# A convolved feed-forward network whose up projection is made token-major and turned back by VectorE and a trip through DRAM

## The chip, the cores and the metric

The kernel runs on one core of a Trainium2 chip. The metric is the device time of one execution in microseconds (us). All weights are read from the chip's memory (DRAM) once, in blocks of 1 MB.

## The reference, cut to what matters

Two transformer blocks act on 256 tokens of width 1024. The part that changes is the convolved feed-forward network at the end of the first block:

```python
def conv_ffn(h, w_up, conv_w, conv_b, w_down):       # h: 256 x 1024, w_up: 1024 x 5632
    u = causal_dwconv(h @ w_up, conv_w) + conv_b     # 3 taps along the tokens, per feature
    a, b = jnp.split(u, 2, axis=-1)                  # 2816 features each
    return (jax.nn.silu(a) * b) @ w_down             # w_down: 2816 x 1024
```

It comes behind memory attention (`mem_o`) and a norm (`norm_ffn`). Behind it come the second block's first gated network (`ffn1`, `down1`), whose up and gate projections have the same sizes but no convolution, a token mixer, a second gated network (`ffn2`, `down2`) and a last projection.

## The kernel before

**Blocks and splits.** Every matrix product is made of three products of two-part numbers: high by high, low by high, high by low. SyncE (the queue SP) loads a weight block of 1 MB in two halves of 512 KB into RAW (two slots). ScalarE copies each half to HI (L1656), VectorE subtracts it to LO (L2238), and TensorE uses HI and LO (rings of four blocks). `PHASES` gives the order of the blocks: `up` has 22, `down` 11. `split_ahead(phase, Turn(j))` on ScalarE and on VectorE makes HI and LO of the block four further on: ScalarE waits until block j has been used (`block_done`) and until the raw half has landed. The load of block n waits until LO of block n-2 exists (`lo_is_ready(sp, phase, t, -RAWS, half)`), and each engine and each queue runs strictly in the order in which its program is written.

**Two ways to multiply.** `f_gemm` is feature-major: the weights are the stationary operand and 256 tokens are moved, so that the result has features on partitions and tokens along the free axis, 48 matmuls of 256 columns for a block. `t_half` and `t_open` are token-major: the tokens are stationary (two tiles of 128) and 512 weight columns are moved, 24 matmuls of 512 columns for a block; two blocks (the halves of the contraction) make a chunk of 512 features, for two banks of PSUM. The convolution runs along the tokens, so it wants the feature-major form.

**up before.** Its first three blocks are computed token-major by `f_open` in a second set of PSUM banks (the first tile of tokens needs no second half of the norm), copied to OPENED and turned by TensorE. The other 19 are feature-major. For each block pair (256 features of a, the same of b), `up_step` does on ScalarE two base activations per block (`L2036`, middle tap and bias), a Silu, and the copy to HH; on VectorE four taps per block (`L2726`, straight from PSUM), a gate product (`L2735`) and the low half HL (`L2712`). Steps from the third on are a hardware loop (`repeat`).

**ffn1, for comparison.** It is token-major (`glu`, `glu_steps`): five chunk pairs of gate and up (20 blocks), then two feature-major blocks. VectorE turns the gated product in blocks of 32x32 into TURNED (L2761), SP sends that to DRAM (`hidden_out`, L620) and brings it back into BLOCKS as four transfers (`hidden_in`, L628), ScalarE copies it to HH and VectorE makes HL (L2768). One such round trip belongs to four weight blocks.

**PSUM.** There are four accumulator banks, ACCP 0 to 3. A chunk takes a pair of them, by turns 0 and 1, or 2 and 3; of the two feature-major blocks at the end of ffn1, the first takes bank 0 and the second bank 3. `down` takes all four, 0 and 1 for the first tile of tokens and 2 and 3 for the second; for its first two blocks PE does both blocks of the first tile before the second tile. `acc_banks_free` on PE waits for whoever reads a bank to say that it is taken.

Of the kernel before, what the change touches and what calls it, by code (L numbers as in the profile page):

```python
# [22 lines left out]
P = 128  # L23
# [51 lines left out]
T_OPEN = {"mix_v": 4, "ple_g": 4, "ffn1": 4, "ffn2": 4}  # L75
F_OPEN = {"up": 3}
# [12 lines left out]
GLUS = ("ffn1", "ffn2")  # L89


def _accumulations():
# [9 lines left out]
    for phase, count in PHASES:  # L102
# [8 lines left out]
        elif phase == "w_out":  # L111
            acc(phase, 0, count - 1, 2, 3, 0, 1)
        elif phase in ("mem_o", "down", "down1", "mix_o", "down2"):
            acc(phase, 0, count - 1, 0, 1, 2, 3)
        elif phase in GLUS:
            for q in range(2 * GLU_CHUNKS):
                acc(phase, q, 2 * q + 1, 2 * (q % 2), 2 * (q % 2) + 1)
            for j in range(GLU_T, count):
                acc(phase, j, j, 3 * (j - GLU_T))
        elif phase == "ple_e":  # L120
            pass
        elif phase == "pool":
            for j in range(4):
                acc(phase, j, 0, j)
        else:
            for j in range(count):
                acc(phase, j, j, (j + (phase == "up") * 2) % 4)
# [13 lines left out]
def open_turns(r, phase):  # L141

    norms = norm_turns(r)
    blocks = [f"{phase}.{t}{b}" for t in range(NT) for b in range((F_OPEN[phase] + 1) // 2)]
    return norms[:2] + blocks[:1] + norms[2:] + blocks[1:]

# [11 lines left out]
SMALL += open_turns("norm_ffn", "up") + norm_turns("norm_f1")  # L160
# [3 lines left out]

BY_BLOCK = {f"{phase}.1{b}": FIRST[phase] + min(2 * b + 2, n) for phase, n in F_OPEN.items() for b in range((n + 1) // 2)}
BY_BLOCK["ple.1b"] = FIRST["ple_e"] + 1
# [35 lines left out]
def build(nc, A, out):  # L202
# [24 lines left out]
    with ctx:  # L227
# [94 lines left out]
        UA = at("UA", 44, [P, 2, 2, SEQ])  # L322
        UB = at("UB", 48, [P, 2, 2, SEQ])
# [4 lines left out]
        OPENED = at("OPENED", 56, [P, NT, 4 * 256])  # L328
# [51 lines left out]
        opened = sem("opened")  # L380
# [26 lines left out]
        a_base, a_act, b_base, h_ready, h_hi, h_lo = sems("a_base a_act b_base h_ready h_hi h_lo")  # L407
        turned, turned_out, blocks_in, blocks_split = sems("turned turned_out blocks_in blocks_split")
        post_sq, tap_done, dve_mix = sems("post_sq tap_done dve_mix")
# [25 lines left out]

        def repeat(eng, first, last, stride, step):


            groups, over = divmod(last - first, stride)
            for j in range(first, first + over):  # L440
                step(Turn(j))
            with eng.Fori(0, groups) as i:
                for j in range(first + over, first + over + stride):
                    step(Turn(j, i, stride))
# [34 lines left out]
        def acc_is_done(eng, phase, t):  # L479

            if t.j < F_OPEN.get(phase, 0):
                before = list(F_OPEN.values())[:list(F_OPEN).index(phase)]
                eng.wait_ge(opened, sum(before) + t.j + 1)
                return
# [24 lines left out]
        def conv_tap(tap, tile, t):  # L509

            return FCONV[:, moved(tap * 2 * FT + tile, t, 2)]

        def conv_bias(tile, t):
            tile_, row = COL_AT["ffn_conv_b"]
            return COL[tile_][:, moved(row + tile, t, 2)]

        def moved(c, t, per_turn):

            return slice(c, c + 1) if t.i is None else bass.ds(c + t.i * (t.stride * per_turn), 1)

        def tiles_of(t):

            return slice(2 * t.j, 2 * t.j + 2) if t.i is None else bass.ds(2 * t.j + t.i * (2 * t.stride), 2)
# [41 lines left out]
        def _(sp):  # L565
# [41 lines left out]
            def load_pairs(phase, first, second):  # L607

                def step(t):
                    at_loop = 0 if t.i is None else t.i * (256 * t.stride)  # L610
                    for k, (m, c) in enumerate((first, second)):
                        load(phase, t.part(k, 2), f_block(m, at_loop + (c + 256 * t.j)))
                repeat(sp, 0, FT // 2, 2, step)

# [7 lines left out]
            def hidden_in(phase, c):  # L622
# [4 lines left out]
                for r in range(4):  # L627
                    sp.dma_start(BLOCKS[32 * r:32 * r + 32].rearrange("p b m k t -> p b (m k t)"),  # L628
                                 hidden_rows[:, :, r, :].rearrange("b f c -> f b c")).then_inc(blocks_in, 16)

# [21 lines left out]

            def load_down(phase, m):
                def step(t):
                    load(phase, t, d_block(m, t.j if t.i is None else t.i * t.stride + t.j))
                repeat(sp, 0, FT // 2, 4, step)
# [57 lines left out]
            load_pairs("up", (w["w_up"], 0), (w["w_up"], DFF))  # L714
            load_down("down", w["w_down"])
# [199 lines left out]
        def _(pe):  # L915
# [147 lines left out]

            def f_open(phase, r):

                n = F_OPEN[phase]
                for t in range(NT):
                    for j in range(n):
                        if t == 0 and j == n - 1:

                            norm_turn(r, XS, 1)
                        name = f"{phase}.{t}{j // 2}"
                        if j % 2 == 0:
                            small_bank_free(pe, name)
                        dst = small(name)[:, j % 2 * 256:j % 2 * 256 + 256]
                        for b in range(2):
                            s = lo_is_ready(pe, phase, Turn(j), half=b)
                            if j == 0:
                                pe.wait_ge(norm_hi, 4 * NORMS.index(r) + 2 * t + b + 1)
                            for k in range(4 * b, 4 * b + 4):  # L1080
                                c = slice(k * 256, (k + 1) * 256)
                                pe.matmul(dst, XH[:, k, tok(t)], HI[:, s, c], start=k == 0, stop=False)  # L1082
                                pe.matmul(dst, XH[:, k, tok(t)], LO[:, s, c], start=False, stop=False)  # L1083
                            if j == 0:
                                small_is_taken(pe, f"{r}.{t}{b}")
                            for k in range(4 * b, 4 * b + 4):
                                c = slice(k * 256, (k + 1) * 256)
                                last = pe.matmul(dst, XL[:, k, tok(t)], HI[:, s, c], start=False, stop=k == KT - 1)  # L1088
                        if t == 1:
                            last.then_inc(block_done, 1)  # L1090
                        elif j % 2 == 1 or j == n - 1:
                            finish(last)
                for j in range(n):
                    acc_banks_free(pe, phase, Turn(j))
                    for t in range(NT):
                        small_is_taken(pe, f"{phase}.{t}{j // 2}")
                    for half in range(2):
                        for t in range(NT):
                            dst = acc(phase, Turn(j))[:, half * SEQ + t * P:half * SEQ + (t + 1) * P]
                            c = j * 256 + half * P  # L1100
                            last = pe.transpose(dst, OPENED[:, t, c:c + P], IDENT[:, :])
                    last.then_inc(opened, 1)
# [390 lines left out]
            def ffn(r, up, down, behind):  # L1493
                def step(t):
                    for k in range(2):
                        f_gemm(up, t.part(k, 2), XH, XL)

                def hidden_ready(k):
                    if up in GLUS and k < 4 * GLU_CHUNKS:
                        pe.wait_ge(blocks_split, NT * (chunks_before(up, k // 4) + 1))  # L1500
                    elif up in GLUS:
                        pe.wait_ge(h_lo, FT // 2 + GLUS.index(up) + 1)
                    else:
                        pe.wait_ge(h_lo, k // 2 + 1)

                if up in GLUS:
                    glu(up, r)
                else:
                    f_open(up, r)
                    for j in range(F_OPEN[up], 4):  # L1510
                        f_gemm(up, Turn(j), XH, XL)
                    repeat(pe, 2, FT // 2, 2, step)
# [120 lines left out]
        def _(act):  # L1633
# [23 lines left out]

            def split_behind(phase, t):

                if t.i is not None or t.j >= 2:  # L1660
                    split_ahead(phase, t)
# [263 lines left out]
            def take_opened(phase, t):  # L1925

                n = F_OPEN.get(phase, 0)
                for b in range((n + 1) // 2):
                    name, width = f"{phase}.{t}{b}", min(2, n - 2 * b) * 256
                    if t == 1 and b < 2:  # L1930
                        split_ahead(phase, Turn(b))
                    if (t, b) != (1, 1):
                        take_small(name, OPENED[:, t, b * 512:b * 512 + width], small(name)[:, 0:width])

# [89 lines left out]
            def ffn_hi(t):  # L2024

                copy(HH[:, tiles_of(t), :], UB[:, t.j % 2], h_hi)

# [996 lines left out]
```

## Time and profile before

| | us |
|---|---|
| median of 3 runs | 1135.3 (1134.24 to 1135.6) |
| profiled execution, its own time | 1133.93 |
| its span, from the first to the last instruction | 1132.0 |
| PE busy | 1123.1 (99%) |
| VectorE busy | 756.8 (67%) |
| ScalarE busy | 588.0 (52%) |
| moved by DMA | 225.78 MB, 199 GB/s over the span |

Busy times are averages over stages with different limits. A duration printed for a matmul includes its way through the array, and consecutive matmuls overlap; the distance between two starts is what a matmul costs. On VectorE and ScalarE too an instruction starts a little before the printed end of the one ahead of it, and the rows of a timeline merge neighbours, with their count behind the x.

### The profile page before, as it was taken

How to read it: one execution, taken by the hardware profiler on the slowest of the kernel's cores; microseconds unless marked ns; L12 is line 12 of the kernel's file. 1: busy time of each engine (PE TensorE's matmuls, PEld its weight loads, DVE VectorE, ACT ScalarE, POOL GpSimd, SP SyncE). 2: the span in 40 equal slices, each digit the busy share in tenths (PEclk: the TensorE clock that was granted, in tenths of full speed). 3: DMA queues.
4: the chain of work that ended last, by engine and by line, in shares of the span. 5: the costliest groups of instructions: out<-in, count | busy, mean ns of one | idle time of the engine just before them, and what ended most of it. 6: DMA issues, size and time to landing. Idle time of an engine off the chain costs nothing.

```text
span 1132.0 us, 15919 instructions
## 1 busy us (share of the span) xinstructions
PE 1123.1 (99%) x6129; PEld 973.1 (86%) x6129; DVE 756.8 (67%) x965; ACT 588.0 (52%) x782; POOL 108.0 (10%) x161
## 2 busy tenths in 40 slices
PE   9999999999999999999999999999999999999997
PEld 8998888888889999988888888888888888888886
DVE  6866687657876887863666564566867566655566
ACT  6765654446465765642554444454654365444453
POOL 6410211000011000000000000200500020000011
PEclk9999999999999999999999999999999999999999
DMA  8743753565644766565488866477856669876642
GB/s 259 204 158 98 226 188 113 167 204 173 218 135 145 235 208 187 176 207 186 156 276 255 246 204 220 146 255 234 256 187 203 225 201 292 242 245 220 213 141 75
DMA packets 129589, 225.78 MB, mean 199 GB/s; under 512 B 12161, under 2 KB 58866, under 8 KB 129523
## 3 DMA queue, kind: packets, MB, share of 16 engines
q1 hardware_dynamic: 125921, 214.37, 59.6%
q10 hardware_dynamic: 3506, 10.49, 2.7%
q8 instruction: 45, 0.74, 0.3%
q0 software_dynamic: 96, 0.01, 0.1%
q14 instruction: 21, 0.17, 0.0%
HBM read 215.80 MB, written 9.04 MB: 199 GB/s over the span
## 4 chain that ended last, share of the span: by engine, by line
PE 93%; DVE 3%; DMA 1%; issue 1%; ACT 1%; POOL 0%; POOLq 0%; DVEq 0%; SPq 0%; ACTq 0%
PE ACCP L918 28%; PE ACCP L920 28%; PE ACCP L919 28%; PE SMP L1135 3%; DVE CONVF L2367 1%; DVE LO L2238 1%; PE SMP L1128 1%; DMA RAW<-in_w_in_dram 1%; DMA X<-in_x_dram 0%; PE SMP L1302 0%; PE SMP L1286 0%; PE SMP L1082 0%; PE SMP L1088 0%; PE SMP L1083 0%; PE SMP L1470 0%
## 5 line engine op out<-in xcount | busy, mean ns | idle before, releaser
L2238 DVE TENSOR_TENSOR LO<-RAW,HI 128x1024 fp32r<-128x1024 f32 x365 | 438.9, 1240 | 209.8 <-ACT HI L1656 205.1
L1656 ACT ACTIVATE HI<-RAW 128x1024 fp32r<-128x1024 f32 x366 | 370.5, 1054 | 274.3 <-PE ACCP L920 232.6
L918 PE MATMUL ACCP<-HI,XH 128*128 128x512 f32 (+1 forms) x776 | 303.2, 391 | 0.0
L920 PE MATMUL ACCP<-HI,XL 128*128 128x512 f32 (+1 forms) x776 | 300.6, 387 | 0.0
L919 PE MATMUL ACCP<-LO,XH 128*128 128x512 f32 (+1 forms) x776 | 300.3, 387 | 0.0
L920 PEld LDWEIGHTS ACCP<-HI,XL 128*128 128x128 f32 x776 | 145.7, 188 | 30.1
L919 PEld LDWEIGHTS ACCP<-LO,XH 128*128 128x128 f32 x776 | 145.8, 188 | 28.7
L918 PEld LDWEIGHTS ACCP<-HI,XH 128*128 128x128 f32 x776 | 145.8, 188 | 28.7
L918 PE MATMUL ACCP<-XH,HI 128*128 128x256 f32 x512 | 145.4, 284 | 0.4 <-DVE CONVF L2367 0.4
L920 PE MATMUL ACCP<-XH,LO 128*128 128x256 f32 x512 | 144.9, 283 | 0.0
L919 PE MATMUL ACCP<-XL,HI 128*128 128x256 f32 x512 | 144.9, 283 | 0.0
L918 PE MATMUL ACCP<-HI,HH 128*128 128x512 f32 x328 | 128.0, 390 | 0.0
L920 PE MATMUL ACCP<-HI,HL 128*128 128x512 f32 x328 | 127.7, 389 | 0.0
L919 PE MATMUL ACCP<-LO,HH 128*128 128x512 f32 x328 | 127.6, 389 | 0.0
L918 PEld LDWEIGHTS ACCP<-XH,HI 128*128 128x128 f32 x512 | 98.2, 192 | 0.7 <-issue 0.5
L919 PEld LDWEIGHTS ACCP<-XL,HI 128*128 128x128 f32 x512 | 98.3, 192 | 0.1
L920 PEld LDWEIGHTS ACCP<-XH,LO 128*128 128x128 f32 x512 | 98.2, 192 | 0.0
L772 POOL TENSOR_SCALAR STAT<-STAT 128x1 f32<-128x1 f32 (+3 forms) x24 | 11.7, 486 | 747.6 <-ACT XS L1922 443.3
L920 PEld LDWEIGHTS ACCP<-HI,HL 128*128 128x128 f32 x328 | 61.6, 188 | 12.9
L918 PEld LDWEIGHTS ACCP<-HI,HH 128*128 128x128 f32 x328 | 61.6, 188 | 12.6
L919 PEld LDWEIGHTS ACCP<-LO,HH 128*128 128x128 f32 x328 | 61.6, 188 | 12.5
L1664 ACT ACTIVATE XH<-SMP 128x512 fp32r<-128x512 f32 x34 | 19.3, 597 | 35.9 <-PE SMP L1135 35.6
(409 smaller groups left out, 1133.1 us busy)
## 6 DMA issues: line engine op xcount, KB each, us to landing
RAW<-in_w_in_dram SPq DMA_DIRECT2D x104, 512.0 KB, 4.6
RAW<-in_w_up_dram SPq DMA_DIRECT2D x44, 512.0 KB, 4.5
RAW<-in_ffn_w_gate_dram SPq DMA_DIRECT2D x44, 512.0 KB, 4.6
RAW<-in_ffn_w_up_dram SPq DMA_DIRECT2D x44, 512.0 KB, 4.6
RAW<-in_ffn_w_down_dram SPq DMA_DIRECT2D x44, 512.0 KB, 4.1
RAW<-in_w_down_dram SPq DMA_DIRECT2D x22, 512.0 KB, 4.0
scratch_hidden<-TURNED SPq DMA_DIRECT2D x10, 512.0 KB, 5.6
BLOCKS<-scratch_hidden SPq DMA_DIRECT2D x40, 128.0 KB, 4.0
```

What stands on the lines that cost most here:

```text
L772: link(pool.tensor_scalar(mean_square, mean_square, EPS, None, ALU.add))
L918: pe.matmul(dst, lhs[0], rhs[0], start=start, stop=False)
L919: pe.matmul(dst, lhs[0], rhs[1], start=False, stop=False)
L920: return pe.matmul(dst, lhs[1], rhs[0], start=False, stop=stop)
L1128: last = pe.matmul(small(name)[:, h * P:(h + 1) * P], lhs, rhs, start=True, stop=True)
L1135: last = pe.transpose(small(name)[:, h * P:(h + 1) * P], source(h), IDENT[:, :])
L1656: act.activation(HI[:, n % RING, half_of(half)], RAW[:, n % RAWS, half, :], ACT.Copy).then_inc(hi_ready, 1)
L1664: act.activation(dst, src, ACT.Copy, scale=scale).then_inc(signal, 1)
L2238: dve.tensor_tensor(LO[:, s, c], RAW[:, n % RAWS, half, :], HI[:, s, c].bitcast(f32), ALU.subtract).then_inc(lo_ready[s], 1)
L2367: ins = dve.scalar_tensor_tensor(out=y, in0=u[:, 0:SEQ - back], scalar=col("gdn_conv", (3 - back) * 12 + tile), in1=y, op0=ALU.mult, op1=A ...
```

## The change

`up` becomes token-major: `T_OPEN` opens it as it opens ffn1, `glu` runs its blocks (20 token-major, in ten chunks, a and b by turns; then two feature-major ones for the last 256 features of each half). `f_open`, OPENED, the turning by TensorE and the hardware loops go. Each of the ten chunks r is turned by VectorE straight out of PSUM (`up_turn`), sent to DRAM behind the load of block 2r+7 and brought back behind the load of block 2r+9 (`up_moves`); ScalarE copies it to PLAIN and makes the base of the convolution from it (`up_take`), VectorE applies the taps in groups of four instructions (`chunk_taps`). Silu, gate product, HH and HL work on a whole chunk of 512 features. UA, UB, PLAIN, UP_TURNED and UP_BLOCKS are double. The work of the last chunks is put between the splits of `down`. Three parameter loads move to later places, for the room that they share. The diff at its core:

```diff
-T_OPEN = {"mix_v": 4, "ple_g": 4, "ffn1": 4, "ffn2": 4}
-F_OPEN = {"up": 3}
+T_OPEN = {"up": 4, "mix_v": 4, "ple_g": 4, "ffn1": 4, "ffn2": 4}
+WIDE = ("up",) + GLUS
...
-        elif phase in GLUS:
+        elif phase in WIDE:
             for q in range(2 * GLU_CHUNKS):
                 acc(phase, q, 2 * q + 1, 2 * (q % 2), 2 * (q % 2) + 1)
             for j in range(GLU_T, count):
...
+            def up_moves(loaded):
+                for r in range(2 * GLU_CHUNKS):
+                    if loaded == 2 * r + 7:
+                        for m in range(NT):
+                            acc_is_taken(sp, "up", Turn(r), m)
+                        wait(sp, up_in[r % 2], 64 * (r // 2))
+                        sp.dma_start(up_rows[r % 2][:, :, :, :].rearrange("b f r c -> (b f) (r c)"),
+                                     UP_TURNED[r % 2][:, :, :, :, :].rearrange("p r m k t -> p (r m k t)")).then_inc(up_out[r % 2], 16)
+                    if loaded == 2 * r + 9:
+                        sp.wait_ge(up_out[r % 2], 16 * (r // 2 + 1))
+                        wait(sp, up_base, r - 1)
+                        for q in range(4):
+                            sp.dma_start(UP_BLOCKS[r % 2][32 * q:32 * q + 32].rearrange("p b m k t -> p b (m k t)"),
+                                         up_rows[r % 2][:, :, q, :].rearrange("b f c -> f b c")).then_inc(up_in[r % 2], 16)
...
# ScalarE
+            def up_take(r):
+                act.wait_ge(up_in[r % 2], 64 * (r // 2 + 1))
+                wait(act, up_taps, 2 * (r - 1))
+                for m in range(NT):
+                    act.activation(PLAIN[r % 2][:, :, tok(m)].rearrange("p k (b t) -> p k b t", b=4),
+                                   UP_BLOCKS[r % 2][:, :, m].rearrange("p b k t -> p k b t"), ACT.Copy)
+                wait(act, up_lo if r % 2 else up_gated, r // 2 - 1)
+                dst = (UA, UB)[r % 2][r // 2 % 2]
+                for i in range(4):
...
+                ins.then_inc(up_base, 1)
+            for c in range(GLU_CHUNKS):
+                split_ahead("up", Turn(4 * c))
+                if c:
+                    up_take(2 * c - 2)
+                split_ahead("up", Turn(4 * c + 1))
+                if c >= 2:
+                    up_hi_copy(c - 2)
+                split_ahead("up", Turn(4 * c + 2))
+                if c:
+                    up_silu(c - 1)
+                    up_take(2 * c - 1)
+                split_ahead("up", Turn(4 * c + 3))
+            last = GLU_CHUNKS - 1
+            rest_base(0)
+            split_ahead("up", Turn(GLU_T))
+            up_take(2 * last)
+            rest_base(1)
+            split_ahead("up", Turn(GLU_T + 1))
...
# VectorE
+            for c in range(GLU_CHUNKS):
+                split_ahead("up", Turn(4 * c))
+                if c >= 2:
+                    chunk_taps(2 * c - 3, 1)
+                    up_gate(c - 2)
+                up_turn(2 * c)
+                split_ahead("up", Turn(4 * c + 1))
+                if c:
+                    chunk_taps(2 * c - 2, 0)
+                split_ahead("up", Turn(4 * c + 2))
+                if c:
+                    chunk_taps(2 * c - 2, 1)
+                if c >= 2:
+                    up_lo_half(c - 2)
+                up_turn(2 * c + 1)
+                split_ahead("up", Turn(4 * c + 3))
+                if c:
+                    chunk_taps(2 * c - 1, 0)
+            last, rest = GLU_CHUNKS - 1, slice(4 * GLU_CHUNKS, FT)
+            rest_conv(0)
+            split_ahead("up", Turn(GLU_T))
+            chunk_taps(2 * last - 1, 1)
+            up_gate(last - 1)
+            rest_conv(1)
+            split_ahead("up", Turn(GLU_T + 1))
+            chunk_taps(2 * last, 0)
```

`up_silu(c)` waits for the taps of chunk 2c, `up_gate(c)` for the Silu and the taps of chunk 2c+1. `rest_base(k)` and `rest_conv(k)` do the convolution of the two feature-major blocks out of PSUM; `rest_conv(k)` frees the bank.

## Rows read from the trace of the kernel before

**Rows 1.** The page: busy time, share and instructions of each engine.

```profile
span 1132.0 us, 15919 instructions
...
PE 1123.1 (99%) x6129; PEld 973.1 (86%) x6129; DVE 756.8 (67%) x965; ACT 588.0 (52%) x782; POOL 108.0 (10%) x161
```

**Rows 2.** PE timeline at up's and ffn1's borders: start, us, instruction.

```profile
355.12 0.36 PE L1082 MATMUL SMP<-HI,XH 128*128 128x256 f32 x1
...
483.63 0.28 PE L919 MATMUL ACCP<-XL,HI 128*128 128x256 f32 x1
...
484.59 0.40 PE L918 MATMUL ACCP<-HI,HH 128*128 128x512 f32 x1
...
545.38 0.39 PE L918 MATMUL ACCP<-HI,XH 128*128 128x512 f32 x1
...
666.59 0.40 PE L918 MATMUL ACCP<-HI,HH 128*128 128x512 f32 x1
```

**Rows 3.** PE timeline inside ffn1, two matmuls 51 places apart.

```profile
559.87 0.39 PE L918 MATMUL ACCP<-HI,XH 128*128 128x512 f32 x1
...
571.43 0.39 PE L918 MATMUL ACCP<-HI,XH 128*128 128x512 f32 x1
```

**Rows 4.** Windows: busy us of each engine, PEclk, DMA share, GB/s.

```profile
380.00:484.00 104.00, 104.00 (x869) 104.00 (x869) 87.11 (x135) 66.23 (x95) 0.00 (x0) 1.00 0.62 197
```

**Rows 5.** VectorE timeline in up, while it is behind and never waits.

```profile
391.63 1.65 DVE L2726 SCALAR_TENSOR_TENSOR UA<-ACCP,FCONV,UA 128x255 f32<-128x255 f32 x4
393.19 2.35 DVE L2238 TENSOR_TENSOR LO<-RAW,HI 128x1024 fp32r<-128x1024 f32 x2
395.46 1.64 DVE L2726 SCALAR_TENSOR_TENSOR UB<-ACCP,FCONV,UB 128x255 f32<-128x255 f32 x4
```

**Rows 6.** VectorE timeline in ffn1: transposes, then the low half.

```profile
593.47 1.30 DVE L2761 STREAM_TRANSPOSE TURNED<-UBT 128x512 f32<-128x512 f32 x2
594.69 1.25 DVE L2768 TENSOR_TENSOR HL<-BLOCKS,HH 128x512 fp32r<-128x512 f32 x2
```

**Rows 7.** Timelines of ScalarE and VectorE: a split, base activations, a take.

```profile
381.52 1.00 ACT L2036 ACTIVATE UA<-ACCP,COL,FCONV 128x256 f32<-128x256 f32 x2
...
584.55 2.01 ACT L1656 ACTIVATE HI<-RAW 128x1024 fp32r<-128x1024 f32 x2 [2.46 <-PE ACCP L920]
...
585.65 2.36 DVE L2238 TENSOR_TENSOR LO<-RAW,HI 128x1024 fp32r<-128x1024 f32 x2 [2.11 <-ACT HI L1656]
...
613.67 1.14 ACT L1664 ACTIVATE HH<-BLOCKS 128x512 fp32r<-128x512 f32 x2
```

**Rows 8.** SP's queue in ffn1: a load's issue (ns), two inward trips.

```profile
L574 SPq DMA_DIRECT2D RAW<-in_ffn_w_up_dram x10: 367/368/390, 597.8 to 637.1; - x10
...
600.44 1.75 SPq L628 DMA_DIRECT2D BLOCKS<-scratch_hidden  x4
...
665.59 1.75 SPq L628 DMA_DIRECT2D BLOCKS<-scratch_hidden  x4
```

**Rows 9.** The last two transfers of each trip, issue to landing.

```profile
L628 SPq DMA_DIRECT2D BLOCKS<-scratch_hidden x2: 432/432/433, 601.3 to 601.8; - x2
DMA to landing us min/median/max: 3.6/3.7/3.8
...
L628 SPq DMA_DIRECT2D BLOCKS<-scratch_hidden x2: 432/432/432, 666.4 to 666.9; - x2
DMA to landing us min/median/max: 4.3/4.9/5.6
```

**Rows 10.** ffn1's opening: HI of its fifth block, LO of its eighth.

```profile
560.07 2.01 ACT L1656 ACTIVATE HI<-RAW 128x1024 fp32r<-128x1024 f32 x2 [4.80 <-PE ACCP L920]
...
572.71 1.22 DVE L2238 TENSOR_TENSOR LO<-RAW,HI 128x1024 fp32r<-128x1024 f32 x1 [0.41 <-ACT HI L1656]
```

**Rows 11.** Windows at the end of the kernel, with the granted clock.

```profile
1125.00:1128.00 3.00, 0.75 (x7) 0.55 (x5) 1.47 (x5) 0.38 (x1) 0.69 (x1) 1.00 0.00 0
1128.00:1131.00 3.00, 0.00 (x0) 0.00 (x0) 1.41 (x2) 0.00 (x0) 0.09 (x1) 0.66 0.42 165
```

More of the change, by code:

```diff
@@ L89 @@
 GLUS = ("ffn1", "ffn2")
+WIDE = ("up",) + GLUS
+TAP_ORDER = [(r, half) for r in range(2 * GLU_CHUNKS) for half in range(2)]
+TAP_ORDER.insert(TAP_ORDER.index((2 * GLU_CHUNKS - 3, 1)), ("rest", 0))
+TAP_ORDER.insert(TAP_ORDER.index((2 * GLU_CHUNKS - 2, 0)), ("rest", 1))
 def _accumulations():
@@ L507, in col, with conv_tap, up_tiles @@
             return COL[tile][:, row + i:row + i + 1]
[L509 to L523, printed above, removed]
+        def conv_tap(tap, tile):
+            return FCONV[:, tap * 2 * FT + tile:tap * 2 * FT + tile + 1]
+        def up_tiles(r):
+            return (r % 2) * FT + (r // 2) * 4
         def lo_is_ready(eng, phase, t, ahead=0, half=1):
@@ L1062, in t_open @@
                             last.then_inc(tile_done, 1)
[L1064 to L1102, printed above, removed]
             def o_part(phase, j, m, ready):
@@ L2739, in _, with taps @@
-            for j in range(2):
-                up_step(Turn(j))
-            repeat(dve, 2, FT // 2, 2, up_step)
+            def taps(u, y, tile, n, done):
+                for back in (1, 2):
+                    for i in range(2):
+                        if back == 2:
+                            dve.wait_ge(up_tap, n + i + 1)
+                        part = y[:, i, back:SEQ]
+                        ins = dve.scalar_tensor_tensor(out=part, in0=u[:, i, 0:SEQ - back], scalar=conv_tap(2 - back, tile + i), in1=part,
+                                                       op0=ALU.mult, op1=ALU.add)
+                        if back == 1:
+                            ins.then_inc(up_tap, 1)
+                ins.then_inc(done, 1)
@@ new lines, in up_turn, with chunk_taps @@
+            def up_turn(r):
+                wait(dve, up_out[r % 2], 16 * (r // 2))
+                acc_is_done(dve, "up", Turn(r))
+                for m in range(NT):
+                    dve.transpose(UP_TURNED[r % 2][:, :, m].rearrange("p r k t -> p k r t"),
+                                  acc("up", Turn(r), m).rearrange("p (k r t) -> p k r t", r=4, t=32)).then_inc(acc_bank("up", Turn(r), m), 1)
+            def chunk_taps(r, half):
+                dve.wait_ge(up_base, r + 1)
+                pair, y = slice(2 * half, 2 * half + 2), (UA, UB)[r % 2][r // 2 % 2]
+                taps(PLAIN[r % 2][:, pair, :], y[:, pair, :], up_tiles(r) + 2 * half, TAP_ORDER.index((r, half)) * 2, up_taps)
@@ new lines, in rest_conv @@
+            def rest_conv(k):
+                b = Turn(GLU_T + k)
+                dve.wait_ge(rest_based, k + 1)
+                taps(acc("up", b).rearrange("p (n s) -> p n s", s=SEQ), UP_REST[k], k * FT + 4 * GLU_CHUNKS,
+                     TAP_ORDER.index(("rest", k)) * 2, rest_taps)
+                dve.wait_ge(rest_taps, k + 1)
+                dve.sem_inc(acc_bank("up", b), 1)
+            for c in range(GLU_CHUNKS):
[16 more added lines that the diff above has]
+                    chunk_taps(2 * c - 1, 0)
```

217 lines of the change are left out of this document (88 added, 129 removed).

## The prediction

> **What bounds the kernel now.** The page comes first: PE is busy for 1123.1 of 1132.0 us [rows 1], so the time is the number of matmuls times their spacing, and every other engine works behind PE. Then the borders of the stage, on PE's timeline: up starts at 355.12 and down at 484.59, so up takes 129.47 us [rows 2]. ffn1's up projection, the same sizes in the token-major form, runs from 545.38 to 666.59, which is 121.21 us [rows 2]. The spacing says why. A 256-column matmul starts every 0.12 us (eight of them between 483.63 and 484.59) [rows 2], so a block of 48 takes 5.76 us. A 512-column one starts every 11.56/51 = 0.2267 us [rows 3], so a block of 24 takes 5.44 us. Last, who is near the limit behind PE: between 380 and 484 us VectorE is busy 87.11 of 104 us, ScalarE 66.23 [rows 4].
>
> **PE's part of the change.** 20 blocks at 5.44 and two at 5.76 give 120.3 us; the turn of the norm's second tile brings ffn1 to 121.21, and up now has the same PE program. If nothing waits, 129.47 - 121.21 = 8.3 us are saved. The opening changes with it: its first blocks are finished only in the second tile's pass.
>
> **The other engines' prices.** The split of a block: ScalarE's first half is followed by VectorE 1.10 us after its start (584.55 to 585.65), both halves on VectorE take 2.36 us, or 2.27 when the same engine goes on (393.19 to 395.46) [rows 5, 7]. Four taps: 391.63 to 393.19, 1.57 us; 1.70 us until another engine hears of it [rows 5]. A pair of transposes: 1.22 us [rows 6]; these read PSUM, which I price the same. A gate product or a low half on 1024 columns is like one LO: 1.135. up_take is two copies (1.14 us printed for such a pair, 1.04 until the next can start) and four bases (two take 1.00 printed, 0.90 to 0.95 with the next behind them), 2.95 us in all with its wait [rows 7]. A Silu on 1024 columns is like one half of HI, 0.95. The taps now read PLAIN in SBUF instead of PSUM, a form not seen here: below, the transposes' price per column would make four of them cost 0.3 us less; above I see no reason for more. I take the old price.
>
> VectorE's sum for a chunk pair (four blocks) is 8 x 1.135 + 4 x 1.57 + 2 x 1.22 + 2 x 1.135 = 20.1 us, and PE needs 4 x 5.44 = 21.8. So it fits in total. What decides is the order.
>
> **The inward trip.** It stands in SP's queue behind the load of block 2r+9, whose second half waits for the second half of LO of block 2r+7. From the end of that LO: 0.05 + 0.37 us to issue the half [rows 8], four transfers of 0.437 us issue each, the last of which starts 1.31 us after the first, and its landing. In ffn1 a trip begun at 600.44 had its last two issues, up to 601.75, landing in at most 3.8 us, so 5.1 us in all; the one begun at 665.59 had 5.6 us from 666.9, so 6.9 us in all [rows 8, 9]. That makes 5.55 to 7.35 us from LO to data. I take 6.5: here the trip always follows a full load at once, as in the slower row.
>
> **The loop.** Call E(c) the end of LO of block 4c+3, which is the last split of iteration c-1. From there the written order gives one chain without a gap:
> - trip of chunk 2c-2: 6.5
> - up_take(2c-2): 2.95 (ScalarE stands in it, and the split of the next block is queued behind)
> - HI to LO: 1.10
> - LO of block 4c+5: 2.27
> - taps: 1.57
> - LO of block 4c+6: 2.27
> - taps, heard by ScalarE: 1.70
> - Silu: 0.95
> - up_take(2c-1): 2.95
> - HI to LO: 1.10
> - LO of block 4c+7, which is E(c+1): 2.36
>
> The sum is 25.7 us. up_take(2c-1) has a trip of its own, behind the load that waits for LO of block 4c+5; 6.5 us from there against 6.40 us of the chain adds 0.1. So the loop takes 25.8 us, and PE's four blocks 21.8. While ScalarE holds the splits back, VectorE idles some 5 us per pair, filled only by a transpose pair and a low half. The loop doesn't depend on PE at all once VectorE lags, and each iteration lags by 4.0 us more. In the kernel before nothing like it exists: base, taps, gate of a block pair have no transfer between them.
>
> **What the lag costs.** All from up's start. In ffn1 HI of the fifth block starts at 560.07 - 545.38 = 14.7, and LO of the eighth ends at 573.93, 28.5 us in [rows 2, 10]; up has similar work there, so E(1) = 28.5. E(4) = 28.5 + 3 x 25.8 = 105.9 and E(5), LO of down's second block, is 131.7. PE's side, without waits: block 3 ends at 14.7 + 3 x 2.72 = 22.8, block 17 at 99.0. The ring of four lets LO of a block come some 16 us after its slot came free (three blocks), and LO is in time up to E(4), wanted at 104.4 and then later. The PSUM banks are what comes late:
> - block 18 needs banks 2 and 3, taken by the turn of chunk 7 at E(4) - 5.0 = 100.9: 1.9 us of wait. Block 19 ends at 111.8.
> - block 20 needs bank 0, the turn of chunk 8 at E(4) + 7.2 = 113.1: 1.3 us. It ends at 118.9.
> - block 21 needs bank 3, the turn of chunk 9 at E(5) - 5.0 = 126.7: 7.8 us. It ends at 132.5.
> - down's first tile needs bank 0 back from rest_conv(0), behind taps and base: E(5) + 3.3 = 135.0: 2.5 us. Two blocks of that tile end at 140.4.
> - its second tile needs bank 3 from rest_conv(1). On ScalarE rest_base(1) stands behind up_take(8), which needs the trip behind the load after E(5): 6.5 + 2.95 + 1.02 + 0.05 + 1.65 + 0.1 = 12.3, so 144.0: 3.6 us. Two blocks of that tile end at 149.4.
>
> The kernel before is at that point at 129.47 + 2 x 5.44 = 140.4. The change is 9.0 us behind there: 8.3 saved, 17.1 waited. In the rest of down VectorE has less than 5.2 us of work in each 5.44 us block, and the last hidden tiles are wanted only at its ninth block, so I cost the leftovers there at nothing (if that cover were gone, at most one low half and a split, 3.4 us). The moved parameter loads are wanted tens of us later and are hidden. The unrolled loops cost nothing: ffn1 is unrolled, and its 121.21 us leave no room for a gap. Nothing behind down gives or takes anything.
>
> So the profiled execution would be 1133.93 + 9.0 = 1142.9; the median of the runs stands 1.4 us above that execution, so 1144.3.
>
> **The clock.** At the kernel's end PE stops at about 1126 us, and the granted clock is 1.00 in the window to 1128 and 0.66 in the next three us, so it falls from 2.4 to 1.2 GHz after an idle time [rows 11]. The wait at block 21 is 7.8 us. At half the clock that block would take up to 5.8 us more and end at 138.3; two blocks of the first tile would then end at 143.7, still before 144.0. So it is covered, and costs at most the matmuls behind it if the clock is still low then, up to 5 us. The Trainium skill ("TensorE: Matmul & The Clock Gate", Part 1: The HAM clock gate) says the throttled clock is the default and only activity lifts it. By that rule each of the short waits behind could keep it down, and the result would be up to those 5 us worse; the rows show only the fall, not the return.
>
> **Rivals.**
> 1. ScalarE and VectorE keep up and PE never waits (faster): the ring and the double buffers absorb all. For it: VectorE's sum is below PE's. Against it: the loop above. It gives 1135.3 - 8.3 = 1127.0 in full for a loop of at most 21.5 us (28.5 + 4 x 21.5 + 12.3 = 126.8, when PE would want bank 3 for down's second tile), and a part of it up to 23.5. Chance 0.13.
> 2. The loop lags, but less: a trip of 5.55 and both groups of taps 0.3 us cheaper give 24.2 and an end 1.6 us behind; with 23.5 to 23.8 the gain and the waits cancel. Same or slightly faster, 1133 to 1137. Chance 0.10.
> 3. The chain as above: chance 0.69. With a trip of 5.55 the loop is 24.8 and the end 4.0 us behind before; with 7.35 both trips count, the loop is 27.5 and the end 16.8 us behind. So 1139.3 to 1152.1.
> 4. Outward trips and loads share the queue and the DMA engines with twice ffn1's trips, and landings get longer than any row shows (8 us and more), or the low clock stays: beyond 1152. Chance 0.08.
>
> **The numbers.** A measurement of this kernel tells about 0.2% from no change, 2.3 us. Faster takes all of rival 1 and 0.04 of rival 2: 0.17. Same takes 0.05 of rival 2 and 0.01 of the third's low end: 0.06. Slower: 0.77. The range reaches down to rival 2 and up just beyond the third: 1134 to 1153, which leaves out 0.13 below and about 0.06 above.
>
> **What would show it.** Right: ffn1's unchanged 121.2 us; up's matmuls at 0.2267 us; PE waiting about 8 us in one piece some 119 us into up for a transpose on UP_TURNED, and shorter before and after; ScalarE's longest waits being for UP_BLOCKS' transfer; LO of blocks 7, 11, 15, 19 ending 25 to 26 us apart; SP's inward trips landing 6 to 7 us after LO. Wrong: LO of those blocks 21.8 us apart (rival 1); VectorE without gaps in up (then its prices are too low here). My weakest number is the trip's: 1 us more or less in it moves the end by 5 us or more.

## The result, and the profile after

The change makes the kernel slower: 1157.64 us (median of 4 runs, 1154.65 to 1158.92) against 1134.8 us in the same batches, a ratio of 1.0197 [1.0176, 1.0218]. That is 22.8 us more; the forecast was 9.0 us more, and its range ended at 1153. The sign and the chain of waits came as predicted, the size did not. The rows below are of an execution of 1157.48 us.

The page after (busy time of each engine; then the shares of the chain that ended last; then two rows of the DMA issues: KB each, median us from issue to landing):

```profile
span 1155.3 us, 14628 instructions
...
PE 1122.6 (97%) x5637; PEld 950.1 (82%) x5637; DVE 767.3 (66%) x974; ACT 596.4 (52%) x789; POOL 107.8 (9%) x161
...
PE 81%; DMA 6%; DVE 6%; ACT 3%; issue 2%; SPq 1%; POOL 0%; POOLq 0%; DVEq 0%; ACTq 0%
...
UP_BLOCKS<-scratch_up SPq DMA_DIRECT2D x40, 128.0 KB, 4.7
scratch_up<-UP_TURNED SPq DMA_DIRECT2D x10, 512.0 KB, 6.4
```

PE's busy time is that of before [rows 1] within half a microsecond, while the span grew by 23.3 us: the time is waiting. The chain of work that ended last now runs through a transfer for 6% of the span.

PE's timeline at the borders of the stage, with PE's waits over 1.5 us at blocks 20 and 21 and at down's second tile (start, duration, and in brackets the idle time before it and what ended it):

```profile
356.28 0.47 PE L913 MATMUL ACCP<-HI,XH 128*128 128x512 f32 x1 [0.36 <-DVE XL L2247]
...
477.43 0.36 PE L913 MATMUL ACCP<-XH,HI 128*128 128x256 f32 x1 [1.73 <-DVE UP_TURNED L2677]
...
492.37 0.56 PE L913 MATMUL ACCP<-XH,HI 128*128 128x256 f32 x1 [8.96 <-DVE UP_TURNED L2677]
...
502.15 0.47 PE L913 MATMUL ACCP<-HI,HH 128*128 128x512 f32 x1 [1.35 <-issue]
...
512.11 0.77 PE L913 MATMUL ACCP<-HI,HH 128*128 128x512 f32 x1 [4.27 <-DVEq L2706]
...
568.86 0.39 PE L913 MATMUL ACCP<-HI,XH 128*128 128x512 f32 x1
```

ffn1 starts at 568.86 instead of 545.38 [rows 2]: 23.5 us later, so all of the loss has arisen by then. The two long waits stand where the forecast put them: 8.96 us in one piece at block 21 (it begins 127 us into up, the forecast had 119), and 4.27 us at down's second tile. Shorter ones, 0.2 to 1.7 us, begin at block 13 already, earlier than forecast.

Who waits for whom between 355 and 540 us (engine, tile and line, what ended the waits; sum in us, count, longest):

```profile
DVE LO L2202 <- ACT HI L1601: 47.6, 15, 6.7
ACT PLAIN L1950 <- DMA UP_BLOCKS<-scratch_up: 40.3, 10, 7.6
...
ACT UA L1964 <- DVE UA L2666: 15.9, 4, 4.1
PE ACCP L913 <- DVE UP_TURNED L2677: 15.4, 5, 9.0
ACT HI L1601 <- DMA RAW<-in_w_up_dram: 6.3, 6, 1.5
```

Read as a chain: PE waits for VectorE's turn, VectorE for ScalarE's HI, and ScalarE, which makes HI, for the inward trip, ten times, 40.3 us in all. Weights are hardly waited for (6.3 us).

One loop of the chain, from the end of LO of block 15 (440.56 + 2.36 = 442.92) on. SP's row, then ScalarE's, then VectorE's:

```profile
443.42 1.84 SPq L616 DMA_DIRECT2D UP_BLOCKS<-scratch_up  x4
```

```profile
449.83 1.15 ACT L1950 ACTIVATE PLAIN<-UP_BLOCKS 128x512 f32<-128x512 f32 x2 [6.47 <-DMA UP_BLOCKS<-scratch_up]
450.89 2.06 ACT L1956 ACTIVATE UA<-UP_BLOCKS,COL,FCONV 128x256 f32<-128x256 f32 x4
452.86 1.99 ACT L1601 ACTIVATE HI<-RAW 128x1024 fp32r<-128x1024 f32 x2
...
461.76 1.06 ACT L1964 ACTIVATE UA<-UA 128x1024 f32<-128x1024 f32 x1 [4.05 <-DVE UA L2666]
...
463.44 1.15 ACT L1950 ACTIVATE PLAIN<-UP_BLOCKS 128x512 f32<-128x512 f32 x2 [0.62 <-DMA UP_BLOCKS<-scratch_up]
```

```profile
440.56 2.36 DVE L2202 TENSOR_TENSOR LO<-RAW,HI 128x1024 fp32r<-128x1024 f32 x2 [3.16 <-ACT HI L1601]
...
453.94 2.36 DVE L2202 TENSOR_TENSOR LO<-RAW,HI 128x1024 fp32r<-128x1024 f32 x2 [3.03 <-ACT HI L1601]
456.22 1.66 DVE L2666 SCALAR_TENSOR_TENSOR UA<-PLAIN,FCONV,UA 128x255 f32<-128x255 f32 x4
457.79 2.35 DVE L2202 TENSOR_TENSOR LO<-RAW,HI 128x1024 fp32r<-128x1024 f32 x2
460.06 1.66 DVE L2666 SCALAR_TENSOR_TENSOR UA<-PLAIN,FCONV,UA 128x255 f32<-128x255 f32 x4
...
467.54 2.36 DVE L2202 TENSOR_TENSOR LO<-RAW,HI 128x1024 fp32r<-128x1024 f32 x2 [3.46 <-ACT HI L1601]
```

The steps are the trip from 442.92 to 449.83 (6.9 us), take (3.03), HI to LO (1.08), LO (2.28), taps (1.57), LO (2.27), taps (1.70), then Silu and a short wait for the second trip (1.68), take (3.02), 1.08 and LO 2.36, ending at 469.90: 27.0 us. This loop had the shortest trip of the four. The LO ends of blocks 7, 11, 15, 19 and 23 are at 385.92, 415.13, 442.92, 469.90 and 498.85: 29.2, 27.8, 27.0 and 28.95 apart, mean 28.2, against the forecast 25.8. The trips from such an end to the take lasted 8.2, 8.0, 6.9, 8.1 and 7.2 us, mean 7.7 against 6.5. The rows of the other LO ends (blocks 7, 11 and 23; start plus duration), and of the other takes:

```profile
384.69 1.23 DVE L2202 TENSOR_TENSOR LO<-RAW,HI 128x1024 fp32r<-128x1024 f32 x1 [0.35 <-ACT HI L1601]
...
412.77 2.36 DVE L2202 TENSOR_TENSOR LO<-RAW,HI 128x1024 fp32r<-128x1024 f32 x2 [5.54 <-ACT HI L1601]
...
496.49 2.36 DVE L2202 TENSOR_TENSOR LO<-RAW,HI 128x1024 fp32r<-128x1024 f32 x2 [4.27 <-ACT HI L1601]
```

```profile
394.11 1.15 ACT L1950 ACTIVATE PLAIN<-UP_BLOCKS 128x512 f32<-128x512 f32 x2 [5.62 <-DMA UP_BLOCKS<-scratch_up]
...
423.15 1.15 ACT L1950 ACTIVATE PLAIN<-UP_BLOCKS 128x512 f32<-128x512 f32 x2 [7.57 <-DMA UP_BLOCKS<-scratch_up]
...
477.98 1.15 ACT L1950 ACTIVATE PLAIN<-UP_BLOCKS 128x512 f32<-128x512 f32 x2 [7.63 <-DMA UP_BLOCKS<-scratch_up]
...
506.08 1.15 ACT L1950 ACTIVATE PLAIN<-UP_BLOCKS 128x512 f32<-128x512 f32 x2 [5.87 <-DMA UP_BLOCKS<-scratch_up]
```

### The profile page after: what moved, and what is told of

It reads as the page before. It is cut to its first block, busy times and chain, and to the rows that moved or that the text cites. A ratio compares the mean times of both kernels' runs of the same rounds, so it can differ in the third digit from the quotient of the medians.

```text
span 1155.3 us, 14628 instructions
## 1 busy us (share of the span) xinstructions
PE 1122.6 (97%) x5637; PEld 950.1 (82%) x5637; DVE 767.3 (66%) x974; ACT 596.4 (52%) x789; POOL 107.8 (9%) x161
## 4 chain that ended last, share of the span: by engine, by line
PE 81%; DMA 6%; DVE 6%; ACT 3%; issue 2%; SPq 1%; POOL 0%; POOLq 0%; DVEq 0%; ACTq 0%
PE ACCP L913 25%; PE ACCP L915 25%; PE ACCP L914 25%; DMA UP_BLOCKS<-scratch_up 4%; DVE LO L2202 3%; PE SMP L1090 3%; DVE CONVF L2326 1%; PE SMP L1083 1%; SPq L616 1%; ACT HI L1601 1%; ACT UA L1956 1%; DMA RAW<-in_w_in_dram 1%; ACT UB L1956 1%; ACT PLAIN L1950 1%; DMA RAW<-in_w_up_dram 0%
## 5 line engine op out<-in xcount | busy, mean ns | idle before, releaser
L913 PE MATMUL ACCP<-HI,XH 128*128 128x512 f32 (+1 forms) x936 | 366.9, 392 | 7.5 <-DVE UP_TURNED L2677 4.8
L915 PE MATMUL ACCP<-HI,XL 128*128 128x512 f32 (+1 forms) x936 | 363.3, 388 | 0.0
L914 PE MATMUL ACCP<-LO,XH 128*128 128x512 f32 (+1 forms) x936 | 363.0, 388 | 0.0
L914 PEld LDWEIGHTS ACCP<-LO,XH 128*128 128x128 f32 x936 | 176.0, 188 | 34.8
L913 PE MATMUL ACCP<-XH,HI 128*128 128x256 f32 x240 | 69.8, 291 | 11.4 <-DVE UP_TURNED L2677 10.7
L914 PE MATMUL ACCP<-XL,HI 128*128 128x256 f32 x240 | 69.1, 288 | 0.0
L915 PE MATMUL ACCP<-XH,LO 128*128 128x256 f32 x240 | 69.1, 288 | 0.0
L913 PEld LDWEIGHTS ACCP<-XH,HI 128*128 128x128 f32 x240 | 47.3, 197 | 12.2 <-issue 12.0
L914 PEld LDWEIGHTS ACCP<-XL,HI 128*128 128x128 f32 x240 | 47.3, 197 | 0.1
L915 PEld LDWEIGHTS ACCP<-XH,LO 128*128 128x128 f32 x240 | 47.2, 197 | 0.0
```

Source lines behind the costliest of these rows:

```text
L913: pe.matmul(dst, lhs[0], rhs[0], start=start, stop=False)
L914: pe.matmul(dst, lhs[0], rhs[1], start=False, stop=False)
L915: return pe.matmul(dst, lhs[1], rhs[0], start=False, stop=stop)
```

## The experiments

The prediction's theory is the chain: in ScalarE's written order a split stands behind each take, so VectorE gets no work while ScalarE waits for a transfer. Rivals on why it cost more than forecast: too much work on the two engines, the outward transfer, the clock, and the place of the trip in SP's queue.

### ScalarE's order alone (e1_order)

```diff
                 split_ahead("up", Turn(4 * c))
+                split_ahead("up", Turn(4 * c + 1))
                 if c:
                     up_take(2 * c - 2)
-                split_ahead("up", Turn(4 * c + 1))
                 if c >= 2:
                     up_hi_copy(c - 2)
                 split_ahead("up", Turn(4 * c + 2))
+                split_ahead("up", Turn(4 * c + 3))
                 if c:
                     up_silu(c - 1)
                     up_take(2 * c - 1)
-                split_ahead("up", Turn(4 * c + 3))
```

> ScalarE's order alone is changed: up_take(2c-2) stands behind the split of block 4c+5, Silu and up_take(2c-1) behind the split of block 4c+7, so no split of a weight block is queued behind a trip. Theory of the loop (trip, take, split, taps and back, 28.2 us per four blocks in the changed kernel): the ends of LO of blocks 7, 11, 15 and 19 come 21.8 us apart, PE waits only at the border to down (about 1 to 4 us, since rest_base(1) still stands behind up_take(8)), and the time is 1128 to 1132 us, 26 to 30 below the changed kernel and 3 to 7 below the kernel before. Rival, VectorE's own work is too much (its prices with waits add up to more than 21.8 us): the ends stay more than 25 us apart and the time stays above 1145. Rival, the doubled traffic itself holds up the loads: the same, with ScalarE's waits moved from UP_BLOCKS to RAW.

Measured: 1131.05 us, a ratio to before of 0.9973 [0.9961, 0.9984]. Not one instruction more or less, and the kernel is 26.6 us faster than the changed one. LO of blocks 11, 15, 19 and 23 ends at 408.31, 430.68, 452.02 and 473.67, so 22.4, 21.3 and 21.7 apart, PE's own pace of 21.8. Behind up's first matmul PE waits twice, for down's two tiles (PE's timeline):

```profile
479.13 0.47 PE L913 MATMUL ACCP<-HI,HH 128*128 128x512 f32 x1 [1.36 <-issue]
...
487.08 0.47 PE L913 MATMUL ACCP<-HI,HH 128*128 128x512 f32 x1 [2.26 <-DVEq L2706]
```

ScalarE still waits for trips (its waits between 355 and 540 us), 13.7 us instead of 40.3, and now mainly for weights:

```profile
ACT HI L1601 <- DMA RAW<-in_w_up_dram: 22.7, 15, 2.9
...
ACT PLAIN L1950 <- DMA UP_BLOCKS<-scratch_up: 13.7, 7, 6.6
```

It follows that the loss was the order: the trip's latency was put between two splits. Too much work is refuted, since the work is the same.

### The inward trip a load earlier (e2_early)

```diff
-                    if loaded == 2 * r + 9:
+                    if loaded == 2 * r + 8:
```

> Only the inward trips stand one load earlier, behind the load of block 2r+8 instead of 2r+9. Theory of the loop: the even chunk's trip then starts some 6 us before the end of LO of block 4c+3 instead of 0.4 behind it, so its 7.7 us in the loop shrink to about 2 and the odd chunk's trip falls out of the loop too; the loop becomes 22 to 23 us, bound by ScalarE and VectorE waiting for each other, and the time is 1127 to 1134 us. SP now waits about 2 us for the outward trip to land, with nothing urgent behind it. Rival, that wait (which the place one load later avoids) holds up the weight loads: RAW is late, the loop stays at 26 us or more and the time above 1145.

Measured: 1134.04 us, 0.9999 [0.9989, 1.0008]: the whole loss is gone, the gain isn't there. The trace is of its slowest execution, 1136.55 us. LO of blocks 11, 15, 19 and 23 now ends at 412.56, 435.99, 459.08 and 482.16, so 23.1 to 23.4 us apart instead of 28.2. The trips hardly count any more: ScalarE waits 2.2 us for them between 355 and 540 us, where it was 40.3. What is left is VectorE waiting for HI (35.6 us) and ScalarE for taps (12.8) and for weights (18.5, where it was 6.3). PE pays at block 21, and 0.76 and 1.45 us more at down's two tiles (PE's timeline):

```profile
477.23 0.36 PE L913 MATMUL ACCP<-XH,HI 128*128 128x256 f32 x1 [4.25 <-DVE UP_TURNED L2677]
```

So "a load later" is what makes this order expensive, and even without the trip's wait this kernel gives PE's 8.3 us away. How much of that is the order and how much the later weights, this run alone doesn't separate; e6_all below has the early trips too, in the other order, and is 3.5 us faster.

### Order, and the last takes behind the rest (e5_order_tail)

This is e1_order, changed to take away its wait at down's second tile:

```diff
+            rest_base(1)
+            split_ahead("up", Turn(GLU_T + 1))
             up_take(2 * last)
-            rest_base(1)
-            split_ahead("up", Turn(GLU_T + 1))
```

> The order of e1_order, and at the border rest_base(1) and the split of block 21 stand before up_take(8). In e1_order PE waited 2.3 us for rest_conv(1) ahead of down's second tile, behind the trip of chunk 8. Theory: that wait goes and the time falls by about 2 us, to 1128.5 to 1129.5. Rival: the splits of down behind it are then late, because up_take(8) comes later, and the time stays at 1131.

Measured: 1127.29 us (1126.5 to 1128.89), 0.994 [0.9926, 0.9954]: faster than both kernels, by 0.6% against the one before. It is 3.8 us faster than e1_order, where 2 were expected, since both of its waits (1.36 and 2.26 us) are gone: behind up's first matmul PE has no wait in up or down (PE's timeline at ffn1's start, and the window that [rows 4] shows of before: us, busy PE, PEld, DVE, ACT, POOL, granted clock, DMA share, GB/s):

```profile
538.08 0.39 PE L913 MATMUL ACCP<-HI,XH 128*128 128x512 f32 x1
```

```profile
380.00:484.00 104.00, 104.00 (x506) 88.07 (x505) 92.24 (x136) 75.93 (x107) 0.00 (x0) 1.00 0.89 293
```

ffn1 starts 7.3 us before the 545.38 of before [rows 2]; up starts 0.8 us later here (355.96 against 355.12) and takes 121.3 us (down's first matmul is at 477.29) where it took 129.5, so 8.1 of PE's 8.3 us are there. VectorE is busy for 92.24 of 104 us where before it was 87.11, and in the changed kernel 70.53: the same window after reads

```profile
380.00:484.00 104.00, 94.54 (x429) 76.30 (x427) 70.53 (x100) 58.83 (x81) 0.00 (x0) 1.00 0.71 233
```

The changed kernel's VectorE has 33 us of gaps in this stretch, though it is the engine with the least room behind PE: that is the picture of an order that waits, and 89% that of one that doesn't.

### Both, with the early trip (e6_all)

e5_order_tail with the edit of e2_early.

> e5_order_tail and the inward trips one load earlier. With no split behind a trip, the loop no longer holds the trip, so an earlier one should bring nothing: within 1.5 us of e5_order_tail. If ScalarE's waits for UP_BLOCKS (13.7 us in e1_order) still cost, it is 2 us or more faster; if SP's wait for the outward landing delays the loads, which ScalarE already waits for, it is slower.

Measured: 1130.51 us, 0.996 [0.9944, 0.9976]: 3.2 us slower than e5_order_tail: not within 1.5 us, but the case in which SP's wait for the outward landing delays the loads. PE waits 0.45, 1.50 and 1.45 us, at block 21 and at down's two tiles. ScalarE's waits for weights between 355 and 540 us, first here, then in e5_order_tail:

```profile
ACT HI L1601 <- DMA RAW<-in_w_up_dram: 27.7, 19, 4.4
```

```profile
ACT HI L1601 <- DMA RAW<-in_w_up_dram: 9.3, 8, 2.3
```

SP stands in its queue for the outward landing, and the loads stand behind it (SP's own waits between 355 and 500 us; e5_order_tail has none of these):

```profile
SPq L616 <- DMA scratch_up<-UP_TURNED: 26.6, 9, 4.6
```

So the right place of the trip depends on the order: in the changed one early is 23.6 us better than late, in the right one late is 3.2 us better than early.

### Outward transfers left out (e3_noout)

```diff
-                        sp.dma_start(up_rows[r % 2]..., UP_TURNED[r % 2]...).then_inc(up_out[r % 2], 16)
+                        if r < 2:
+                            sp.dma_start(up_rows[r % 2]..., UP_TURNED[r % 2]...).then_inc(up_out[r % 2], 16)
```

The waits on these transfers are set to match. What the kernel leaves out is the sending of chunks 2 to 9, so it multiplies values of chunks 0 and 1 in their place.

> Chunks 2 to 9 are not sent out to DRAM: their inward trips bring back what chunks 0 and 1 left there, so up's hidden values are those of other chunks. Everything else stays. It asks why a trip took 7.7 us from LO to data instead of the 6.5 forecast. If the outward 512 KB share the engines with the inward trip that was issued just before it, the landing of the last inward piece falls from 4.9 to 6.3 us to about 4 to 4.5, the trips to about 6.2 to 6.7 us, the loop from 28.2 to about 26, and the profiled time by 7 to 10 us, to 1147 to 1150. If it is the weight load ahead of it, nothing falls by more than 0.3 us per trip and the time stays within 3 us of the changed kernel's.

Measured, one execution: 1161.01 us. The inward transfers land in 4.1, 4.7 and 7.2 us (shortest, median, longest; 4.3, 4.7 and 6.3 with the outward ones), and the LO ends of blocks 11, 15, 19 and 23 are at 413.68, 441.13, 470.65 and 500.64, 27.5 to 30.0 apart. From such an end to the take passed 7.1, 7.3, 7.5, 8.4 and 8.1 us, mean 7.7 as in the changed kernel. In this one execution the outward transfer doesn't lengthen the trip.

### The clock kept up (e4_warm)

```diff
                 f_gemm(phase, Turn(GLU_T), XH, XL)
+                if phase == "up":
+                    keep_warm(36)
                 f_gemm(phase, Turn(GLU_T + 1), XH, XL)
...
                 for m in range(NT):
+                    if down == "down" and m == 1:
+                        keep_warm(18)
...
+            def keep_warm(times):
+                for _ in range(times):
+                    pe.matmul(SMP[:, SMALL_ORDER["norm_f1.00"] % 4, :], XH[:, 0, tok(0)], XH[:, 0:2, :], start=True, stop=True)
```

The clock of the changed kernel, in windows (columns as above):

```profile
487.00:488.00 1.00, 0.00 (x0) 0.00 (x0) 1.00 (x2) 0.00 (x0) 0.00 (x0) 0.84 0.88 333
...
492.40:494.00 1.60, 1.60 (x7) 1.60 (x8) 0.00 (x0) 1.60 (x4) 0.00 (x0) 0.50 0.85 348
...
498.00:500.00 2.00, 2.00 (x19) 2.00 (x18) 2.00 (x5) 2.00 (x3) 0.00 (x0) 1.00 0.57 129
...
513.00:514.00 1.00, 1.00 (x4) 0.72 (x4) 1.00 (x2) 0.46 (x1) 0.00 (x0) 0.50 0.00 0
...
515.00:516.00 1.00, 1.00 (x6) 0.83 (x5) 0.88 (x3) 0.00 (x0) 0.00 (x0) 1.00 0.91 373
```

PE had been idle since 483.4 when the clock fell from 2.4 to 1.2 GHz at about 487.7; block 21 began at 492.37 in the low clock and had the full one back at about 497.9, so it took 8.4 us instead of the 5.8 at 2.4 GHz. The Trainium skill ("TensorE: Matmul & The Clock Gate", Part 1: The HAM clock gate) says that activity releases the throttle; the trace agrees, the low clock ended some 5.5 us into block 21's matmuls.

> PE multiplies into a spare bank while it would wait: 36 matmuls of 512 columns (about 8.2 us) ahead of block 21 and 18 (4.1 us) ahead of down's second tile; their results are not used. It prices the clock's two falls. Theory: the granted clock stays at 1.00, block 21 takes 5.8 instead of 8.4 us but down's first tile waits for rest_conv(0) all the same, and only the second fall's 1.4 us come back: 1155 to 1157 us. Rival, the clock is what made the wait larger than forecast (two falls, 4 us in all): 1153 or less.

Measured: 1158.13 us, 1.0211 [1.0194, 1.0228], no better, and above the 1155 to 1157 expected. Block 21 now ran at the full clock (first window below), but down's first tile began at 502.81 where it had begun at 502.15, since it waits for VectorE; and in that wait, 4.58 us long, the clock fell instead (second window):

```profile
492.00:498.00 6.00, 5.75 (x48) 5.79 (x48) 0.95 (x2) 4.95 (x9) 0.00 (x0) 1.00 0.37 140
...
503.00:506.00 3.00, 3.00 (x8) 2.32 (x9) 3.00 (x5) 0.00 (x0) 0.00 (x0) 0.50 0.99 300
```

```profile
502.81 0.77 PE L913 MATMUL ACCP<-HI,HH 128*128 128x512 f32 x1 [4.58 <-issue]
...
509.87 4.24 PE L1442 MATMUL SMP<-XH 128*128 128x512 f32 x18
...
513.95 0.39 PE L913 MATMUL ACCP<-HI,HH 128*128 128x512 f32 x1
```

The fall in block 21 is off the path: the forecast's "it is covered" is shown. The dummies ahead of down's second tile ran from 509.87 to 514.1, past the moment when the bank came free, and pushed that tile to 513.95, so the time did not get shorter. But the run prices the second fall: from this tile's start to ffn1's took 55.3 us here, at the full clock (513.95 to 569.28), and 56.75 in the changed kernel (512.11 to 568.86), so the low clock costs 1.4 us there.

### The trip ahead of the second half of its load (e7_ahead)

The changed kernel's order, and its waits; only in SP's queue the trips' transfers, the four inward and the outward ones, stand ahead of the second half of the load that they used to follow:

```diff
-            def load(phase, t, source):
+            def load(phase, t, source, between=None):
...
                         lo_is_ready(sp, phase, t, -RAWS, half)
+                    if half == 1 and between:
+                        between()
...
-                    load("up", Turn(j), t_block(...))
-                    up_moves(j)
+                    load("up", Turn(j), t_block(...), lambda: up_moves(j))
```

> The changed kernel with one thing moved: the trips are issued ahead of the second half of their load instead of behind it; the wait on LO that starts them is the same. Leaving the outward trips out did not shorten the inward ones, so the load issued just ahead is left as what makes them 7.7 us instead of the 6.5 forecast. Theory: the last inward piece lands 1 to 1.5 us sooner, the loop falls from 28.2 to about 25.5 to 26.5, and the time by 8 to 12 us, to 1146 to 1150. Rival, the trip is as long by itself (reading back from DRAM what was just written, in pieces of 1 KB): no change beyond 3 us.

Measured: 1141.8 us, 1.0061 [1.0045, 1.0078], 15.8 us faster than the changed kernel, where 8 to 12 were expected; the rival, no change beyond 3 us, is refuted. The trace is of an execution of 1143.14 us. A loop that answers to the one above (LO of block 15 ends at 435.08), SP's row and then ScalarE's:

```profile
435.11 1.75 SPq L618 DMA_DIRECT2D UP_BLOCKS<-scratch_up  x4
```

```profile
441.36 1.15 ACT L1949 ACTIVATE PLAIN<-UP_BLOCKS 128x512 f32<-128x512 f32 x2 [5.82 <-DMA UP_BLOCKS<-scratch_up]
...
454.25 1.13 ACT L1949 ACTIVATE PLAIN<-UP_BLOCKS 128x512 f32<-128x512 f32 x2
```

From LO to the take passed 4.1, 5.2, 6.3, 5.2 and 5.1 us, mean 5.2 instead of 7.7, and the second take has no wait left. Of these 2.5 us some 0.4 are the issue of the half, which is no longer ahead [rows 8]; the rest is that the last of the four transfers reaches its reader 3.8 us from its issue instead of 5.8, on the mean of these five trips (over all 40 transfers the median landing is 3.7 instead of 4.7 us, the longest 5.3 instead of 6.3). The 512 KB are no longer ahead of them, and the outward transfer, which moved too, makes no difference in e3_noout. The LO ends stand 24.7 us apart instead of 28.2, which is 14.2 us over four loops; ffn1 starts 15.3 us sooner (553.57). The prediction's sum with 5.2 in place of 6.5 and no second wait gives 24.4. The Trainium skill ("DMA: Bandwidth & Descriptors", Queues, rings and completion order) says that each DMA engine takes the descriptors of one queue in their order; these runs agree, with 7.7 us behind the half and 5.2 ahead of it.

### The opening (e8_opening)

e5_order_tail, with the first tile's first two blocks of up using XH ahead of XL, for the 0.36 us that the first matmul waits for XL:

```diff
+                        if phase == "up" and m == 0 and j < 2:
+                            first_part(r, j)
+                            continue
                         last = t_part(phase, j, m, XH, XL, norm_ready(r, m), by_half=m == 0)
```

> e5_order_tail with the first tile's first two blocks in the old opening's product order: both products with XH first, the product with XL last, so that PE starts before VectorE has made XL. In the changed kernel up starts 1.2 us later than before, 0.4 of it a wait for XL. Theory: 0.4 to 1 us less than e5_order_tail. Rival: the later start came from ahead of up (loads, norm), and nothing changes.

Measured: 1126.92 us (1125.75 to 1129.37), 0.9936 [0.9922, 0.995]. It isn't told apart from e5_order_tail; up starts 0.22 us sooner (355.74 against 355.96). Inconclusive.

## Why the prediction was right in kind and wrong in size

- **PE's part**: right. ffn1's form and spacing hold for up; 8.1 of the 8.3 us came as soon as nothing waited (e5_order_tail: 7.3 us at ffn1's start, and 0.8 used up by up's later start; up took 121.3 us there, ffn1's 121.2 in the forecast).
- **The loop**: right in every term but the trip. Take 3.03 for 2.95, HI to LO 1.08 for 1.10, LO 2.27, taps 1.57 and 1.70 are as put down; that taps read from SBUF cost what they did from PSUM, which was a choice, held too.
- **The step that failed is "The inward trip", "I take 6.5"**: it measured 7.7 on average. The second trip, which the loop counted with 0.1 us, took 8.1, 6.85, 7.1 and 8.0 us from its LO against the chain's 6.40, and cost 1.56, 0.33, 0.62 and 1.44 us. Together the four loops are 112.9 us instead of 103.2: 9.7 of the excess. The bounds came from ffn1's rows [rows 8, 9], where a trip comes once in four blocks; here the last piece landed 4.9 to 6.3 us from its issue where those rows allow 3.8 and 5.6. The value taken was low even for ffn1: in the kernel before, the slowest pieces of its five trips landed 5.3, 3.8, 5.5, 4.6 and 5.6 us from issue, and their mean, 5.0, in the prediction's sum (0.42 + 1.31 + 5.0) gives 6.7 us. e7_ahead shows that the 512 KB half ahead in the queue makes up some 2.5 us of the trip; e3_noout shows no part for the outward transfer. Why ffn1's trips are shorter stays open: the prediction's reason for its value, that the trip follows a full load at once, doesn't sort them, since of those five the one issued 0.1 us behind its load's second half landed in 4.6 us, and one issued 2.9 us behind it in 5.3.
- **The start and the end of the chain**: LO of block 7 came 29.6 us after up's start for 28.5 (1.1), down's second tile 13.26 us after LO of block 23 for 12.3 (1.0, most of it the trip again), and up itself began 1.2 us later.
- **The clock**: "covered" at block 21 is shown by e4_warm. The low clock in down's second tile adds about 1.4 us. e4_warm prices it. It was foreseen as a possibility and put in the sum at nothing, the second step that failed.
- **The account**: 9.0 forecast + 1.2 start + 1.1 + 9.7 + 1.0 + 1.4 = 23.4; ffn1 starts 23.5 us late. That it adds up is arithmetic from one trace; of its parts, the loop's excess and the 1.4 have an experiment behind them, up's later start, the 1.1 and the 1.0 have none.
- **The waits of PE**: 8.96 for 7.8 at block 21 and 4.27 for 3.6 at the second tile; 1.73 for 1.3 at block 20 and 1.35 for 2.5 at the first tile. But they began at block 13 (1.28 us before 429.67, for LO), 72 us into up, where the forecast had the first at block 18, 99 us in: the lag grew by 6.4 us a loop instead of 4.0.
- **The rivals**: the first was wrong for this order and right for another. e1_order nearly reached its loop of 21.5 us (mean 21.8), and e5_order_tail, in that order, ran at its time (1127.29 for 1127.0). The fourth, beyond 1152, held the result, though no transfer's landing took the 8 us and more that it was built on (the longest was 6.3); an average trip 1.2 us over the value taken was enough. "1 us more or less in it moves the end by 5 us or more" was the right warning, and a range that ended at a 7.35 us trip had no room for a mean above the slowest row.

## What to carry to other kernels

An instruction that waits for a transfer must not stand ahead of work that another engine needs: count the latency into the loop by the written order of every in-order engine, since sums of busy time will say that all fits. A small transfer that somebody waits for did better ahead of a large one released by the same signal in the same queue (5.2 us instead of 7.7), and whether it should be issued earlier still depends on who stands behind it in that queue. A latency that recurs in every loop should be bounded by more than two rows, with room above the slowest.

## What the runs showed of the hardware beyond what was expected

- Four transfers of 128 KB right behind a 512 KB one in the same queue reached their reader 7.7 us after the common release; ahead of it 5.2 us (e7_ahead), their median landing 3.7 instead of 4.7 us from issue, the last of the four 3.8 instead of 5.8 on the mean of five trips.
- Leaving out the 512 KB outward transfers of the same queue changed nothing in that landing in one execution (median 4.7 both times, the longest 7.2 us without them and 6.3 with them).
- In the changed kernel TensorE's granted clock fell from 1.00 to 0.50 (2.4 to 1.2 GHz) with PE idle since 483.4, at about 487.7, and was 1.00 again at about 497.9, after some 5.5 us of dense matmuls; it fell again at about 511.6, within the 4.27 us wait, and was back at about 515, some 2.9 us after the matmuls had begun again. With the first wait filled by matmuls it fell shortly before 503 instead, within the 4.58 us wait ahead of down's first tile.
